# Seven block products for eight in the up projection of a ConvFFN, and a down projection in a pass of its own

## The reference

```
u = rmsnorm(x, norm_ffn) @ ffn_w_up                     # 1024 -> 2 x 2816
u_pad = concatenate([buf0, u], axis=1)                   # two rows of history
uc = sum(u_pad[:, j:j + T] * wc[j] for j in range(3)) + ffn_conv_b
gate, up = split(uc, 2, axis=-1)
x = x + (silu(gate) * up) @ ffn_w_down                   # 2816 -> 1024
new_buf = u_pad[:, -2:]                                  # an output
```

## Time and profile before

| | us |
|---|---|
| median of 3 runs (lowest, highest) | 3063.3 (3061.11, 3065.82) |
| profiled execution, whole | 3064.34 |
| its span in the profile | 3062.5 |
| mean granted clock of TensorE | 0.982 |
| TensorE busy | 2942.2 (96%) |
| VectorE busy | 1581.2 (52%) |
| ScalarE busy | 1136.7 (37%) |
| GpSimd busy | 141.3 (5%) |

### The profile page before, as it was taken

One profiled execution on the slowest core, in us unless ns is written; L12 is line 12 of the kernel. 1 busy time (PEld: TensorE's weight loads), 2 busy tenths in 40 slices (PEclk: granted clock), 3 DMA queues, 4 the chain that ended last, 5 costly groups with the idle time before them and its releaser, 6 DMA issues. The chain is left out here.

```text
span 3062.5 us, 46703 instructions
## 1 busy us (share of the span) xinstructions
PE 2942.2 (96%) x19219; PEld 2779.4 (91%) x19219; DVE 1581.2 (52%) x2699; ACT 1136.7 (37%) x2151; POOL 141.3 (5%) x260
## 2 busy tenths in 40 slices
PE   6999989999999999999989998899999999999997
PEld 5998745999999999999989986569999999999997
DVE  5234644664544555457661446455645554455665
ACT  6233333543333223335452342344432233333353
POOL 0000300000000000000000003000000000000000
PEclk9999999999999999999999989999999999999998
DMA  3101153321111111112221022533211111111121
GB/s 131 42 28 68 73 172 118 140 74 42 44 54 42 42 55 42 56 47 83 91 72 42 17 107 84 162 103 126 74 42 42 56 42 56 42 42 46 43 98 70
DMA packets 70742, 215.40 MB, mean 70 GB/s; under 512 B 6522, under 2 KB 43386, under 8 KB 54146
## 3 DMA queue, kind: packets, MB, share of 16 engines
q1 hardware_dynamic: 70530, 212.42, 20.1%
HBM read 193.52 MB, written 18.87 MB: 69 GB/s over the span
## 5 line engine op out<-in xcount | busy, mean ns | idle before, releaser
L236 PE MATMUL psum<-h_chunk,out_weight_parts 128*128 128x352 f32 x2112 | 681.5, 323 | 0.0
L237 PE MATMUL psum<-h_chunk,out_weight_parts 128*128 128x352 f32 x2112 | 677.1, 321 | 0.0
L238 PE MATMUL psum<-h_chunk,out_weight_parts 128*128 128x352 f32 x2112 | 676.4, 320 | 0.0
L2257 DVE SCALAR_TENSOR_TENSOR conv_sum<-u_padded,vectors,conv_sum 128x1024 f32<-128x1024 f32 x176 | 226.3, 1286 | 540.5 <-ACT conv_sum L2109 537.4
L237 PEld LDWEIGHTS psum<-h_chunk,out_weight_parts 128*128 128x128 f32 x2112 | 396.8, 188 | 0.0
L236 PEld LDWEIGHTS psum<-h_chunk,out_weight_parts 128*128 128x128 f32 x2112 | 396.2, 188 | 0.0
L238 PEld LDWEIGHTS psum<-h_chunk,out_weight_parts 128*128 128x128 f32 x2112 | 395.8, 187 | 0.0
L236 PE MATMUL psum<-g_parts,out_weight_parts 128*128 128x352 f32 x960 | 309.3, 322 | 0.0
L237 PE MATMUL psum<-g_parts,out_weight_parts 128*128 128x352 f32 x960 | 309.0, 322 | 0.0
L238 PE MATMUL psum<-g_parts,out_weight_parts 128*128 128x352 f32 x960 | 308.8, 322 | 0.0
L2283 DVE TENSOR_TENSOR x<-x,psum 128x352 f32<-128x352 f32 x528 | 254.8, 519 | 94.4 <-PE psum L238 94.1
(11 more groups left out here) (360 smaller groups left out, 5420.9 us busy)
## 6 DMA issues: line engine op xcount, KB each, us to landing
out_weight_stage<-w_up_dram SPq DMA_DIRECT2D x44, 1024.0 KB, 4.7
out_weight_stage<-w_down_dram SPq DMA_DIRECT2D x22, 1024.0 KB, 4.7
mix_weight_stage<-w_in_dram SPq DMA_DIRECT2D x18, 1024.0 KB, 4.9
pages<-cache_dram SPq DMA_DIRECT2D x64, 288.0 KB, 4.3
out_weight_stage<-w_out_dram SPq DMA_DIRECT2D x16, 1024.0 KB, 6.8
out_weight_stage<-w_gate_dram SPq DMA_DIRECT2D x16, 1024.0 KB, 4.7
pages<-cache_dram SPq DMA_DIRECT2D x64, 160.0 KB, 2.6
x<-x_in_dram SPq DMA_DIRECT2D x6, 1408.0 KB, 11.2
```

The source lines that it names most:

```text
L236: pe.matmul(out, lhs[0], rhs[0], start=first, stop=False)
L237: pe.matmul(out, lhs[0], rhs[1], start=False, stop=False)
L238: return pe.matmul(out, lhs[1], rhs[0], start=False, stop=last)
L2257: dve.scalar_tensor_tensor(t[:, q, 0:SEQ], row[:, tap:tap + SEQ], w, t[:, q, 0:SEQ], ALU.mult, ALU.add).then_inc(ph["conv_step"], 1)
```

## The change

**Up projection.** The product of the weights (512 + 512 input features by gate and up of a feature tile) with the activations (512 + 512 input features by 528 + 528 columns) is taken as a 2 x 2 block product and made with seven block products in place of eight (the Winograd form). Four combinations T1 to T4 of activation blocks are made once a layer, four sums S1 to S4 of weight blocks (A11, A12, A21, A22) once for each feature tile. The first feature tile is still made directly, while the T blocks are being made. A block product has k = 512 and 528 columns, in two halves of 264: 2 x 4 x 3 = 24 matmuls. The results are combined on VectorE (`u2`, `u3`, corners `c22`, `c21`, `c12`) and, for the corner that needs only TensorE's own sums, copied by ScalarE (`m1`, `corner`). `u` has two buffers, `t` one.

**X and g in DRAM.** The T sums overwrite `X`, so the residual is stored to DRAM in four pieces during the projection, scaled in place, and read back at the end of the up pass. The gated rows g of each feature tile are stored to DRAM and read back in thirds of the columns, in groups of three feature tiles.

**Down projection.** It is a pass of its own behind all up tiles: for each third c, 16 units of 11 k tiles (33 matmuls of 352 columns); each unit's weights are loaded, once for each third, into five slots.

**Attention scores.** Where a block has two slices of keys, the matmuls of both slices without rope come first, then those with rope.

**Other.** The slab of SBUF grows from 50304 to 54144 words, with a smaller scratch for dynamic DMA; the host lays out the up and down weights in the new order.

The core of the diff (new functions and the new orders; waits on semaphores kept where they matter):

```
 def out_conv:
+  product_order(f): (A11, S3, S1, A12, S2, A22, S4) if f == 1 else (A11, S3, S2, S1, A12, A22, S4)
+  UNIT_ORDER = 0, 2, 1, 3, *range(4, 2 * KX)
+  G_GROUPS = [(k, min(k + 3, LAST)) for k in range(0, LAST, 3)]
 sync:
+  for f in range(1, LAST):
+      store_g(f - 1)                       # waits g_made >= f; 128 x 1056 f32
+      if f + 2 < FT:
+          sp.wait_ge(ph["m_done"], m_before(f) + 12)
+          load_up(f + 2)
...
+  # last tile: load_g groups 0..6 and load_down 0..4 between its products, then
+  for c in range(NC): X third c back from DRAM
+  store_g(LAST); conv_out
+  for n in range(8 * NC): load_down(2n+5), load_down(2n+6); load_g of the next third
+  load_down(n): if n >= 5: sp.wait_ge(ph["half_done"], n - 4 + 1)
 scalar:
+  history(0); first_evacuate(0..3); sums_high(1); t_high(T1); t_high(T3); first_evacuate(4, 5)
+  t_high(T2); first_evacuate(6, 7); t_high(T4); taps(0, 1); taps(0, 0)
+  for f in range(1, FT):
+      m1(f); blocks_high(f + 1)            # last tile: g_high(0, 0), g_high(0, 1)
+      if f > 1: silu(f - 1)
+      sums_high(f + 1)                     # last tile: down_high(0), (1), g_high(0, 2), (0, 3)
+      history(f); corner(f)
+      if f == 1: silu(0)
+      # waits c21_made, c22_made >= 2f
+      taps(f, 1)
+      # waits c12_made, c11_made >= 2f
+      taps(f, 0)
+  def taps(f, q):
+      if f: act.wait_ge(ph["g_stored"][(f - 1) % 2], 16 * ((f - 1) // 2 + 1))
+      act.activation(t[:, q, 0:SEQ], row[:, 2:US], ACT.Identity, bias=bias, scale=w2)
+      (and the same for the 32 sample columns)
 vector:
+  scales and lows of third 2; weight_sums(1); blocks_low(1); t_sum(T1); t_sum(T3); sums_low(1)
+  t_low(T3); t_sum(T2); t_low(T1); t_sum(T4); t_low(T2); t_low(T4)
+  u2(1, 0); u2(1, 1); u3(1, 0); u3(1, 1); c22(1, 0); c22(1, 1); weight_sums(2); blocks_low(2)
+  conv(0, 1, 0); conv(0, 1, 1); c21(1, 0); c21(1, 1); sums_low(2); c12(1, 0); c12(1, 1)
+  conv(0, 0, 0); conv(0, 0, 1)
+  for f in range(2, FT):
+      if f == 2: gated(0)
+      conv(f - 1, 1, 0); conv(f - 1, 1, 1)
+      if f < LAST: weight_sums(f + 1)
+      u2(f, 0); conv(f - 1, 0, 0); u2(f, 1); conv(f - 1, 0, 1); u3(f, 0); u3(f, 1)
+      blocks_low(f + 1)                    # last tile: g_low(0, 0)
+      c22(f, 0); c22(f, 1); gated(f - 1)
+      sums_low(f + 1)                      # last tile: g_low(0, 1); down_low(0)
+      c21(f, 0); c21(f, 1); c12(f, 0); c12(f, 1)   # last tile: g_low(0, 2), down_low(1) between
+  g_low(0, 3); conv(LAST, 1, 0); conv(LAST, 1, 1); g_low(0, 4); conv(LAST, 0, 0); conv(LAST, 0, 1)
+  g_low(0, 5); down_low(2); gated(LAST); g_low(0, 6); low of g[LAST]; down_low(3)
+  for n in range(8 * NC):
+      add_down(n); square n - 1; down_low(2n+4); down_low(2n+5); g_low of the next third
+  def weight_sums(f):                      # four sums of 128 x 512
+      if f >= 3: dve.wait_ge(ph["m_done"], m_before(f - 1))
+      S1 = A21 + A22; S2 = S1 - A11; S3 = A11 - A21; S4 = A12 - S2
+  t_sum(T): two subtractions of 128 x 1056 in X; t_low(T): one of 128 x 2112
+  blocks_low: 128 x 1536; sums_low: 128 x 2048
+  u2: part2 += S2's bank; u3: part3 = part2 + S3's bank; corners: u = part + bank (128 x 264)
 tensor:
+  first(g), g = 0..7: direct products on column slices of 264, 264, 176, 352, gate and up
+  for f in range(1, FT): seven products, two halves each; waits:
+      A11: blocks_low(f); S3: sums_low(f), T3's low; S1: T1's low; S2: T2's low; A22: T4's low
+      A12: m1(f); A22: u3(f); S4: c22(f); each bank free of tile f - 1
+  def product(f, i, s, a, x, begin):
+      for k in range(KH):
+          pe.matmul(out, w[0], parts[0], ...); pe.matmul(out, w[0], parts[1], ...)
+          mm = pe.matmul(out, w[1], parts[0], ...)
+  for d in range(2 * KX * NC): down(d)     # waits wd_lo_made, glo_made (first output tile), x_made
 mla_attend, scores(p):
-                for c in range(0, keys, 512):
-                    for b in range(2): matmul(ps[2b + c//512], qn, kn)      # start
-                    for b in range(2): matmul(ps[2b + c//512], qr, kr)      # stop
+                for c, w in slices: for b in range(2): matmul(..., qn, kn)  # start
+                for c, w in slices: for b in range(2): matmul(..., qr, kr)  # stop
```

More of the change, by code:

```diff
@@ L2022, in _ @@
               .then_inc(ph["hist_loaded"], 16)
[L2023 to L2030, removed]
+            sp.wait_ge(ph["m_done"], FIRST_G)
@@ new lines, in c22, with c21, c12 @@
+            def c22(f, s):
+                dve.wait_ge(ph["u3_made"], 2 * (f - 1) + s + 1)
+                if f >= 2 and s == 0:
+                    dve.wait_ge(ph["tail_made"], f - 1)
+                    dve.wait_ge(ph["conv_step"], 8 * (f - 1))
+                corner(f, s, 1, 1, part3, bank(3, s), S1, "c22_made")
+            def c21(f, s):
+                corner(f, s, 1, 0, part2, bank(2, s), A22, "c21_made")
+            def c12(f, s):
+                corner(f, s, 0, 1, part2, bank(3, s), S4, "c12_made")
@@ L2361, in _ @@
[L2361 to L2370 removed]
+            for k in range(0, KH):
+                scale(2, k)
@@ new lines, in _ @@
+            low(2, (0,))
+            for k in range(KH, KH + 2):
+                scale(2, k)
+            low(2, (2,))
+            for k in range(KH + 2, KX):
+                scale(2, k)
+            low(2, (4,))
+            low(2, (6,))
+            weight_sums(1)
+            blocks_low(1)
+            t_sum(T1)
+            t_sum(T3)
+            sums_low(1)
+            t_low(T3)
+            t_sum(T2)
+            t_low(T1)
+            t_sum(T4)
+            t_low(T2)
+            t_low(T4)
@@ L2372, in _ @@
+            down_low(3)
+            for n in range(8 * NC):
+                c, i = divmod(n, 8)
+                add_down(n)
+                if n:
+                    end_squares.add(dve, n - 1)
+                for d in (2 * n + 4, 2 * n + 5):
+                    if d < 16 * NC:
+                        down_low(d)
+                if c < NC - 1 and i < len(G_GROUPS):
+                    g_low(c + 1, i)
+            end_squares.add(dve, 8 * NC - 1)
         @block.tensor
@@ new lines, in product @@
+            def product(f, i, s, a, x, begin):
+                at, out = slice(s * SUB, (s + 1) * SUB), bank(i, s)
+                for k in range(KH):
+                    w = [unit(slot_of(f), a, q, k) for q in range(2)]
+                    parts = [part[:, k, at] for part in x]
+                    pe.matmul(out, w[0], parts[0], start=begin and k == 0, stop=False, skip_group_check=not begin)
+                    pe.matmul(out, w[0], parts[1], start=False, stop=False, skip_group_check=not begin)
+                    mm = pe.matmul(out, w[1], parts[0], start=False, stop=k == KH - 1, skip_group_check=not begin)
+                mm.then_inc(ph["m_done"], 1)
```

855 lines of the change are left out of this document (591 added, 264 removed).

## The result

| | before | after | after less before |
|---|---|---|---|
| median (lowest, highest), 4 runs each, us | 3063.06 (3061.11, 3065.82) | 3024.47 (3023.84, 3027.98) | -38.6 |
| profiled execution; span, us | 3064.34; 3062.5 | 3027.98; 3026.2 | -36.3 in the span |
| mean granted clock | 0.982 | 0.976 | |

The ratio after to before is 0.9876, 95% interval 0.9859 to 0.9893. Forecast were 3005 with a range of 2984 to 3046.

The account below looks back on a forecast made before the run. Matmul spacing on TensorE was taken as the bound. Per layer, 48.7 us less matmul work, minus losses of 16.7 (start), 2.2 (up to down) and 2.5 (clock), gave -29.1; two layers -58, so 3005 us, range 2984 to 3046.

Parts of the forecast that it names:

- the start's chain: Start of the up pass, until A22 of tile 2 may start at 721.1 instead of 704.4: loss 16.7 us a layer.
- 1.8 earlier as the matmuls ahead of it are shorter: First up tile, layer 0: VectorE gets its norm row at 653.3 instead of 655.08.
- ends S2 at 687.8; DVE makes u2, u3, c22 by 689.9: Tile 1 of the up pass, layer 0: TensorE finishes product S2, then VectorE its adds and corner, at these times.
- The first wait: From up to down, before the third down unit: TensorE waits 2.2 us a layer, bounds 0 and 6.
- a unit ... lands after about 3.9: Down pass: 704 KB weight load, with splitting 9 us of 10.5 a pair, covered with 1.5 us to spare.
- Rival (4): Down pass late at its units: landings 2 us slower cost 0.5 on each of 48 pairs; 3029 us, chance 0.07.
- The clock: After TensorE's idles at tile 2, half the work at 1.2 GHz: 2.5 us a layer, between 0 and 5.
- One change of kind less ... in 16 score pairs is at most 3 us gained: Attention scores, non-rope matmuls of two slices together: about 0.2 us per change of kind, entered in the forecast at nothing.
- (1): VectorE paces the up pass: a tile takes some 21.3 us, 30 us more, 3035 us; chance 0.20.
- (2): Up pass: ring through the store of g, 18.8 us; with a 7.5 us store, tiles take 22.8, total 3093; chance 0.10.
- (3): Start of the up pass costs less, 10 instead of 16.7 us and no clock loss: 2987 us; chance 0.10.
- (5): Up products: large fixed part of a matmul's spacing, 110 ns cancelling the saved columns; over 3100 us, chance 0.01.

Follow-up runs that it names:

- nine sums: Changed kernel with the first weight sum made nine times instead of once on VectorE from feature tile 4 on; 3152.4 us.
- five: Changed kernel with the first weight sum made five times instead of once on VectorE from feature tile 4 on; 3047.2 us in one run.
- the later store: Changed kernel with SyncE's queue, from tile 4 on, asking for the weights of the tile after next before storing g; 3096.9 us in one run.

## Why the prediction was right or wrong

**Right: what carries the sign.** The spacing of 122.2 ns (122.3), tiles of 20.47 us (20.55), VectorE at 83% (84%), PE without idle from tile 3 to the end of the up pass. From A22 of tile 2 to the down pass it took 396.9 us, 396.4 forecast. The saving of the seventh product came in full, about 49 us a layer, and was then partly spent.

**Wrong: the start's chain was followed on one engine.** From the first up matmul to A22 of tile 2 it took 84.2 us against 75.4 forecast, 8.8 more. VectorE got its norm row at 655.84 and not at 653.3, 2.5 us of it. The step that failed there is "1.8 earlier as the matmuls ahead of it are shorter": the sums that the row needs did not become earlier with the matmuls, since VectorE's last sum of squares paces them (TensorE's wait of 1.43 us in the rows above), and behind them 3.4 us at the lower clock cost another 1.4. (Counted from the first up matmul, which came 0.65 us earlier, the row is 3.2 late.) The rest is the step "ends S2 at 687.8; DVE makes u2, u3, c22 by 689.9": c22 ended at 698.9, because A12 stands ahead of S2 in TensorE's order for tile 1 and waits for `m1`, and `m1` is behind T4's high part and two taps rows in ScalarE's queue; 5.6 us came by it. The prediction laid out that order for VectorE and TensorE and took ScalarE's share as inside it. From there on all its steps came at the forecast distance: g 8.6 us late, taps 8.5, A22 of tile 2 8.1. Moving `m1` gave 12.0 us of stretch back in two layers.

**Wrong: the down pass was covered on average, not at the boundary.** It took 261.5 us against 256.6. The first wait was smaller than forecast, 1.49 for 2.2, but "a unit ... lands after about 3.9" did not ask what SyncE's queue does when the next third's g is also in it. 4.2 us of idle and 1.5 of clock came there, 0.8 at the boundary before; and away from the waits the matmuls follow at 160.1 ns on average and not 159, 1.7 us over the pass. Rival (4) had the right place and a wrong form: not every pair late, but one queue position a layer.

**The clock.** Forecast 2.5 us a layer. In layer 0's stretch some 20 us pass at 1.2 GHz, against none before; 10 of them lie ahead of 722. Counting the matmuls in these spells at their slower spacing, I put 1.4 us of the late norm row to it, 1.5 behind the wait for `m1` in tile 1 (which makes S2 and u3 later still), 2.0 behind the wait of A22 in tile 2 and 1.5 behind unit 20; the spell behind S3's wait in tile 2 falls ahead of waits that would have been there anyway. That makes 6.4, an attribution by place that no run isolated.

**Wrong the other way: attention.** "One change of kind less ... in 16 score pairs is at most 3 us gained" miscounted. A pair had three changes between the two kinds and now has one, two less, and 0.40 us is what the pair gained: 0.2 for each, as estimated, times two. It hid how far the ConvFFN part was off: with the old scores the kernel is at 3035.8, 27 us under the 3062.8 that the kernel before took on the same chip, not 58.

**Rivals.** (1) did not happen: VectorE waited 3.5 us in each period. Its sum was off too: 17.2 + 2.3 + 1.3 is 20.8 and not 21.3, hardly over the period. (2) did not, but it is what stands nearest: 2.5 us of slack, measured with nine sums and confirmed with five, and used up by the later store. (3) and (5) did not. Of the prediction's small errors, 5.22 us between the rows of 256 columns is 5.24 by the rows shown; nothing hangs on it.

**Open.** Two profiled executions of the old scores show the ConvFFN stretch 2 to 3 us longer (716.6, 716.3 in layer 0) than the changed kernel's two (713.6, 714.3), though its code is the same. Their waits at tile 1 are the same, and the time between them is longer; where the low clock falls differs. That the one makes the other was not shown.

## What to carry to other kernels

When a stage is opened by a chain over several engines, write down each engine's queue for it, not only that of the busiest: a 0.6 us copy, whose input was ready at 677, stood behind a high part and two rows that nobody needed yet, and cost 12 us over the two layers. When an in-order queue serves two streams, look at the step where both are due, since a mean slack says nothing of it, and the better order can differ from one boundary to the next. A ring through memory (make, store, overwrite) is a bound of its own and wants its slack measured: 5.8 us more a tile inside this one, of which 2.5 were slack, cost 128 us over 36 tiles.

## What the hardware showed that I had not expected

TensorE at its lower level took 220 ns for 264 columns (and 293 for 352, behind unit 20), which is columns / 1.2 GHz with no fixed part, where at the full clock 12 ns stand above 264 / 2.4; so the low clock costs a factor of 1.8 in this stream and not 2. Rows of A12 in tile 1, behind the wait:

```profile
690.23 0.42 PE L2829 MATMUL psum<-h_b,block_units 128*128 128x264 f32 x1
690.45 0.42 PE L2830 MATMUL psum<-h_b,block_units 128*128 128x264 f32 x1
690.67 0.42 PE L2831 MATMUL psum<-h_b,block_units 128*128 128x264 f32 x1
```

And a store of 528 KB took 3.2 us from its issue to the first instruction that needed it when it was queued ahead of the weights, and 6.8 us behind 1 MB of them.
